# Expert layers: which TensorE product hands a slot of the weights' ring back

## The reference, cut to what matters

```
scores = sigmoid(h @ w_router); idx = top_k(scores + e_bias, 8)
wts = scores[idx] / sum * 2.5
for each expert e, for the rows that chose it:
    a = silu(xb @ w_gate[e]) * (xb @ w_up[e])
    y += wts * (a @ w_down[e])
y += (silu(h @ s_gate) * (h @ s_up)) @ s_down
```

## Time and profile before

| what | value |
|---|---|
| runs | 3669.88, 3678.89, 3679.59 us; median 3678.89 |
| the profiled execution's own time | 3669.65 us |
| its span, first to last instruction | 3667.9 us |
| mean granted TensorE clock | 0.964 of full speed |
| PE busy | 3331.9 us, 91% of the span, 14420 matmul instructions |
| DVE, ACT, POOL busy | 38%, 15%, 11% |
| moved by DMA | 860.80 MB, mean 235 GB/s |
| ring pieces of the whole program | 618, of which 384 in the expert layers |
| first and last ring load of the expert layers issued (L701) | 2032.7 and 3605.1 us |

### The profile page before, as it was taken

The page is one execution under the profiler, slowest core; times in us unless marked ns, Lnnn a source line. Parts: engine busy times, 40 slices in busy tenths (PEclk is TensorE's granted clock), DMA queues, the critical chain, the costliest instruction groups (busy, mean ns, idle before and its releaser), DMA issues.

```text
span 3667.9 us, 40285 instructions
## 1 busy us (share of the span) xinstructions
PE 3331.9 (91%) x14420; PEld 2243.3 (61%) x14420; DVE 1382.3 (38%) x3103; ACT 536.2 (15%) x1122; POOL 401.7 (11%) x455
## 2 busy tenths in 40 slices
PE   7799989999999999899998988999995998999997
PEld 4688877888888887778564433444343675333333
DVE  5566525555025664665353322222213033111112
ACT  2210112001011003100132111111111022111111
POOL 0000011001010000000113111211112002000000
PEclk8899999999999999999998999999997999999999
DMA  7477533774436762565200689999992215999984
GB/s 285 185 300 297 218 115 146 298 269 154 154 115 243 285 228 94 192 235 214 75 29 0 221 287 389 376 357 357 351 363 84 80 69 217 369 409 367 417 363 178
DMA packets 136451, 860.80 MB, mean 235 GB/s; under 512 B 21712, under 2 KB 25168, under 8 KB 38736
## 3 DMA queue, kind: packets, MB, share of 16 engines
q1 hardware_dynamic: 94992, 672.18, 46.8%
q0 software_dynamic: 40560, 185.13, 14.7%
q10 hardware_dynamic: 720, 1.13, 0.1%
HBM read 849.95 MB, written 36.18 MB: 242 GB/s over the span
## 4 chain that ended last, share of the span: by engine, by line
PE 71%; DMA 14%; DVE 8%; issue 4%; ACT 1%; SPq 1%; POOL 0%; POOLq 0%; DVEq 0%; ACTq 0%
PE ps L745 15%; PE ps L1102 11%; PE ps L1341 10%; DMA ring<-stream_in 9%; PE ps L1083 8%; PE ps L841 7%; PE ps L1363 6%; DMA arena<-mod_stream_in 3%; PE ps L1379 3%; DVE arena L1852 2%; PE ps L1310 2%; DMA moe_out<-arena,slot_token 1%; PE ps L1278 1%; PE ps L757 1%; PE ps L800 1%
## 5 line engine op out<-in xcount | busy, mean ns | idle before, releaser
L1341 PE MATMUL ps<-ring,arena 128*64 128x512 f32 (+2 forms) x2112 | 611.4, 623 | 76.9 <-DMA ring<-stream_in 76.8
L1341 PEld LDWEIGHTS ps<-ring,arena 128*64 128x64 f32 (+2 forms) x2112 | 221.9, 156 | 407.2 <-issue 405.2
L1852 DVE SCALAR_TENSOR_TENSOR arena<-arena,cond 128x512 f32<-128x512 f32 x602 | 426.5, 748 | 84.3 <-DMA arena<-mod_stream_in 75.3
L1102 PE MATMUL ps<-arena,ring 128*128 128x256 f32 x2048 | 451.9, 383 | 3.7 <-DVE arena L2168 3.7
L1102 PEld LDWEIGHTS ps<-arena,ring 128*128 128x128 f32 x2048 | 393.0, 193 | 58.5 <-issue 4.4
L1083 PE MATMUL ps<-H,ring 128*128 128x256 f32 x1920 | 421.9, 380 | 0.2
L1083 PEld LDWEIGHTS ps<-H,ring 128*128 128x128 f32 x1920 | 363.9, 191 | 50.1 <-issue 1.6
L1363 PE MATMUL ps<-ring,arena 128*64 128x512 f32 (+2 forms) x1056 | 309.7, 600 | 19.1 <-DMA ring<-stream_in 11.7
L1520 ACT ACTIVATE arena<-ps 128x512 f32<-128x512 f32 (+2 forms) x358 | 182.1, 509 | 828.3 <-PE ps L745 326.5
L2373 DVE TENSOR_TENSOR arena<-arena,ps 128x256 f32<-128x256 f32 x83 | 34.9, 421 | 646.3 <-ACT arena L1743 646.3
L1363 PEld LDWEIGHTS ps<-ring,arena 128*64 128x64 f32 (+2 forms) x1056 | 103.6, 150 | 193.7 <-issue 173.3
(11 more groups left out here) (275 smaller groups left out, 3280.0 us busy)
## 6 DMA issues: line engine op xcount, KB each, us to landing
ring<-stream_in SPq DMA_DIRECT2D x618, 1024.0 KB, 9.2
arena<-mod_stream_in POOLq DMA_DIRECT2D x124, 1024.0 KB, 5.1
YS<-mod_stream_in SPq DMA_DIRECT2D x12, 1024.0 KB, 4.8
arena<-mod_stream_in SPq DMA_DIRECT2D x8, 1024.0 KB, 13.1
moe_out<-zeros POOLq DMA_DIRECT2D x10, 256.0 KB, 5.7
moe_in<-YS POOLq DMA_DIRECT2D x1, 2048.0 KB, 9.4
moe_out<-arena POOLq DMA_DIRECT2D x1, 2048.0 KB, 8.2
YS<-moe_out POOLq DMA_DIRECT2D x1, 2048.0 KB, 18.4
```

The lines of the kernel that those rows point to most:

```text
L1102: m = mm(out[:, i * T:(i + 1) * T], w[:, c * P:(c + 1) * P], f_h[:, 16 * half + c, :], start=(half == c == 0), stop=(half == 1 and c == 15))
L1341: m = mm(out[at, :], e_xt[:, k % 2, 4 * part + c, at], w[:, c * TC:(c + 1) * TC], start=(part == c == 0), stop=(part == 1 and c == 3))
L1852: ins = stt(acc, w, x, acc, MUL, ADD)
```

## The change

The signal on `piece_used` moves to the last product that reads the piece, where that product carries no other signal. The plan no longer lists which pieces were freed by the step before; it notes for each piece the last round that reads it. A new function `used_up` is called on the products with c = 3 of both parts of `gate_up`, and on those with c = 1 of the second down half. If the round is the piece's last, the product gets the signal itself, unless the part is 1 or 2 and the lane is the round's last one: that product has the PSUM bank's signal, so its slot goes to `done`, and `freeing` hangs it on an early product of the next step as before. No instruction is added, removed or moved on any engine, and SyncE's program is the same. Each slot is still handed back as often as before.

```diff
--- before.py
+++ after.py
@@ -257,12 +257,12 @@
             steps += [(k + 1, 0), (k + 1, 1)] if k + 1 < n else []
             steps.append((k, 2))
         self.order, last = [], {}
-        for at, (k, part) in enumerate(steps):
+        for k, part in steps:
             for r in rounds[k].ranks:
                 if (r, part) not in self.order:
                     self.order.append((r, part))
-                last[r, part] = at
-        self.freed = {step: [self.order.index(w) for w in self.order if last[w] == at - 1] for at, step in enumerate(steps)}
+                last[r, part] = k
+        self.last = last
         self.cap = [max(rd.first + P // len(rd.ranks) for rd in rounds if r in rd.ranks) for r in range(EXPERTS)]
         assert sorted(self.order) == [(r, part) for r in range(EXPERTS) for part in range(3)]
 
@@ -1317,7 +1317,6 @@
                         p = ph.first + plan_.order.index((r, part))
                         pe.wait_ge(piece_full[p % SLOTS], 16 * (p // SLOTS + 1))
                         views.append(ring[:, p % SLOTS, :])
-                    done.extend(piece_used[(ph.first + j) % SLOTS] for j in plan_.freed[k, part])
                     return views
 
                 done = [piece_used[(ph.first - 1) % SLOTS]]
@@ -1326,6 +1325,15 @@
 
                     if done:
                         m.then_inc(done.pop(0), 1)
+
+                def used_up(k, part, r, m):
+
+                    if plan_.last[r, part] == k:
+                        free = piece_used[(ph.first + plan_.order.index((r, part))) % SLOTS]
+                        if part and r == rounds[k].ranks[-1]:
+                            done.append(free)
+                        else:
+                            m.then_inc(free, 1)
 
                 def gate_up(k):
 
@@ -1342,6 +1350,8 @@
                                        start=(part == c == 0), stop=(part == 1 and c == 3))
                                 if c < 3:
                                     freeing(m)
+                                else:
+                                    used_up(k, part, r, m)
                     m.then_inc(full, 1)
 
                 def hidden_turned(k):
@@ -1364,6 +1374,8 @@
                                    start=(c == 0), stop=(c == 1))
                             if c == 0:
                                 freeing(m)
+                            elif half:
+                                used_up(k, 2, r, m)
                     m.then_inc(full, 1)
 
                 def summed_rows(k, half):
```

## The result

The changed kernel takes 3646.9 us (median of 5 runs, 3643.2 to 3656.5) against 3675.0 (5 runs, 3669.9 to 3679.6) for the kernel before. The ratio is 0.9929, 95% interval 0.9911 to 0.9947: some 26 us or 0.7% faster (the two medians lie 28.1 us apart). Forecast were 3646 us and a range of 3630 to 3667. Three more comparisons of the same two kernels gave 0.9932, 0.9931 and 0.9926, with medians of 3651.5, 3650.4 and 3647.5 us for the changed one. Over all of them the changed kernel's 21 runs have a median of 3650.0, and the some 50 runs of the kernel before that stand beside all the kernels here have 3675.

A forecast was written before the change was run, and what follows sets the result against it. TensorE's ring waits in the expert layers bound the possible gain at 88.5 us. First layer 9.0 plus second 19.1 gave 28.1 off 3669.65, 3641.6, with half of 9.2 added 3646 us; range 3630 to 3660, to 3667 with rivals.

The forecast's parts named there:

- saturated stretch: First expert layer from 2215 us on, never short of pieces: its 44.6 us of ring waits stay as they are.
- five waits: Waits ahead of part 1: the second layer's three quads (rounds of four experts) and rounds 4 and 9 of the first.
- Step (b): Part 1 and 2 pieces, except the round's last expert's, freed by their own last product; 9.4 us at second-layer quads.
- The clock: Second layer's three parts 1, some products at 1.2 GHz: shorter waits win 3.4 us, 60% of the 5.7 lost.
- The six down waits: Second layer's down steps behind quads (L1363): all 6.3 us of ring waits go, ends 3 and 6.3.
- step (a): Part 0 pieces freed by their own last product, not part 1's first products: 0.9 us earlier, plus any wait between.
- The first layer: Rounds 4 and 9 win 3.5 and 4 us, two waits between them 1.5; 9.0 us in all, ends 3.7 and 11.
- half step: Half of the 9.2 us between two levels of earlier runs, added since the new median may fall on either.
- Rival 1: Second piece's latency comes from shared engines and stays: five long waits win 1.1 us each, 10 us total; chance 0.12.
- Rival 2: Second layer has no room, 386 GB/s being its ceiling: only the first layer's 9 us stays, 3661 us; chance 0.05.
- Rival 3: Nothing moves, as pieces waited for last belong to last lanes or single experts: 3670 to 3679 us; chance 0.06.
- Rival 4: Slower: first layer's row gathers come late, 1 us in each of 36 rounds, 3678 us; chance 0.04.

The follow-up runs named there:

- fewer bytes: Against the changed kernel, first-layer ring loads from piece 34 on leave out their last quarter (outputs wrong): 3585.6 us, ratio to before 0.9755.

## Why the prediction was right

**Where the time could come from: right.** The forecast left the 44.6 us of the saturated stretch alone and took its gain from five waits and what hangs on them. The stretch kept 44.3, and with fewer bytes and the same signals its waits vanished.

**Step (b), the second piece of two on the first one's place: right.** It goes out 1.24 us behind part 0's start at all three quads, where it had gone out 2.35 behind, and at the first one part 1 starts 6.2 us behind part 0 instead of 9.5. Forecast for the three quads were 9.4 us off 17.0; measured 6.2 in the first profile, and 6.7, 9.2 and 7.1 in the three later ones of the changed kernel. The term was sized with 4.8 us of latency for a load with nothing ahead of it; 4.8 to 4.9 held at the first quad, 5.5 and 7.3 at the others, and in the third of the four profiles 4.8 to 5.0 at all of them.

**The clock, 3.4 us of gain: failed in size.** The three parts 1 last 5.34, 6.31 and 5.34 us, together 17.0, where they had lasted 16.6: no gain. In the three later profiles they took 15.1, 14.3 and 15.4, so that the mean gain over the four is 1.2 us, and the sign named for it (each under 5 us) was met by one part 1 in each of the later three. Two windows of after show why, first the end of the first quad's wait and then the products behind it (the granted clock is the third figure from the right):

```profile
3193.70:3196.20 2.50, 0.00 (x0) 0.01 (x1) 0.00 (x0) 0.00 (x0) 0.00 (x0) 1.00 0.99 403
...
3196.30:3201.50 5.20, 5.20 (x34) 1.49 (x33) 0.00 (x0) 0.00 (x0) 0.00 (x0) 0.67 1.02 427
```

Before, the clock had fallen within the wait, to a mean of 0.73. Now it is full to the end of this wait and falls only behind it, to 1.2 GHz for much of part 1. (At the second quad, with its wait of 4.99 us, it still fell within the wait.) Over the twelve profiles with (b) 28 quad waits were shorter than 3 us, and 12 of them had a part 1 of 3.64 us behind them. That is 43%, where I had taken 60.

**The six down waits, 6.3 us: right,** and shown to be step (a)'s work (1.3 us were left in one of the four profiles). **The second layer in all** was forecast at 19.1; the four profiles of the changed kernel took 516.9, 515.9, 511.3 and 514.4 us against 530.8, on average 16.2 less than the one profile of before.

**The first layer, 9.0 us: right within 2.** Its stretch took 628.7, 631.3, 628.4 and 630.2 against 637.1, on average 7.5 less. The waits of rounds 4 and 9 went to 4.03 and 4.20, that is 3.1 and 3.2 off where 3.5 and 4 were taken. Round 9 had 4.0 to 4.2 in all four profiles, but round 4 had 6.07 in the second and 5.25 in the fourth. In the first profile round 4's last load went out 1.3 us behind part 0's start and took 6.3 us, the upper of the two latencies that the prediction chose between.

Together 16.2 + 7.5 = 23.7 against the sum's 28.1, and against the 25 to 27 us of the four ratios. That the median lies within 1 us of the forecast is thus partly luck. The terms were 2 to 4 us too large, most of it the clock and the second quad, and the median of these first five runs, 3646.9, is the lowest of the four and 3 us under the 3650.0 of all 21. The half step of 4.6 us took nothing back: it puts the kernel before at 3674.3, which is where its runs lie (median 3675). The reason given for it doesn't hold, though. The runs of before have no two levels: with more of them they fill 3664 to 3685 us. The range has a slip too: its own terms give 3637 and 3663 where the prediction has 3634 and 3660, apparently since downwards it takes off the clock's whole 5.7 us. The result lies within either.

**The rivals.** Rival 1 (the second piece keeps its latency) holds in the second quad, in three of the four profiles; round 4 of the second profile, with 1.1 us off its wait, is like it. Rival 2 falls: the layer's mean rose to 398 GB/s. By the figure of about 358 GB/s for a core's HBM, half of a stack's 716, in the Trainium skill's "DMA: Bandwidth & Descriptors", section "Specifications", neither that nor 386 could be; the traces decide against it as a ceiling here. Rival 3 falls with the result. Rival 4 falls: the one late gather of the first layer came in round 1, where it is waited for in every profile, 2.0 us before and 3.3 with the first layer's old signals, and in the saturated stretch none was waited for.

## What to carry to other kernels

Before moving a hand-back signal, ask of each wait which buffer's signal issued the load that ended it, and whether the DMAs had anything else to do at that moment: only where they were idle did an earlier signal pay here, and there it also brings forward the loads queued behind it in order. Where the carrier is taken (here the last lane's product), the free one of two neighbours already brings the other forward by one place in the queue. Judge such a change by the stretches it touches, since 10 us of spread elsewhere hid nearly half of it in a single pair of profiles.

## What the runs showed of the hardware

A wait cut from 5.85 to 2.6 us didn't bring the full clock back for the products behind it: of 28 quad waits between 1.4 and 2.8 us, 16 had products at the lower clock behind them. In 15 of these the clock was 1.00 to the end of the wait and fell afterwards, in one it fell 0.3 us before the end. The three shortest waits, 1.45 to 1.68 us, kept the full clock. And one load of 1 MB with fifteen of sixteen landing signals in after 4.7 us can wait for the sixteenth until 7.3.
